# When feature blocks are loaded in a two-layer MLP by seven products, and the order of the last piece's copies, adds and squares

## The chip, the cores and the metric

The kernel runs on one core of one Trainium2 chip. The metric is the device time of one execution in microseconds (us); the figure given for a kernel is the median of its runs, and a separate execution is taken with the hardware profiler.

## What is computed

One inference step of a one-layer hybrid decoder trunk, for a prompt of 512 tokens and 8 sample tokens, 520 tokens in all, with D_MODEL = 2048. The change touches the last third of it, the MLP and the final norm:

```python
xm = rmsnorm(h, p['norm_mlp_g'])
h = h + jnp.square(jax.nn.relu(xm @ p['w_up'])) @ p['w_down']
...
y_prompt = rmsnorm(hp, final_norm_g)
y_sample = rmsnorm(hs, final_norm_g)
```

W_up is 2048 x 8192 and W_down 8192 x 2048, both float32. Ahead of it, and not touched, come the input projection, four mixers, W_out, cross attention and W_o.

## The kernel before, in words

**Precision.** A float32 product is made from three float32r products: each operand is split in a high part (ScalarE copies it to float32r: `whi`, `xbh`) and a low part (VectorE subtracts the high part from the operand: `wlo`, `xbl`), and TensorE runs high by high, low by high and high by low.

**The down stage.** The hidden features are cut in eight chunks p of 1024 features (`N_CHUNK`), and the 2048 outputs in four strips g of 512 (`GROUPS`). One group G = 4p + g multiplies one chunk by one strip, so there are 32 groups (`N_GROUP`). In a group both matrices are seen as 2 x 2 quarters, and seven products of sums of quarters (`down_product(G, o)`, o = 0 to 6, 24 matmuls each, 168 in a group) take the place of eight. The four quarters of the result are called corners; they are collected in `cbuf`, and GpSimd's queue adds a finished group to `hscr` in HBM with an accumulating DMA (not for the last chunk, whose groups are added on the chip).

**Feature blocks.** The sums of quarters of the hidden features are the same for the four groups of a chunk. They lie in HBM (`hidd`), seven blocks of 520 KB in a chunk, one for each product. `load_block(p, k)` (L903) loads block k of chunk p on SP's queue to one of two sets of buffers (set p % 2). `block_hi` (L1657, ScalarE) makes its high part, `block_lo` (L3330, VectorE) its low part. In chunk p these splits are made for chunk p + 1: block 0 in the group g = 0, blocks 1 and 2 in g = 1, 3 and 4 in g = 2, 5 and 6 in g = 3 (the lists `blocks`, L1710 and L3378). A set may be written once the products of the chunk two before are done with it.

**Weight pieces.** Each group needs four quarters of its piece of W_down, `load_down(G, r)` (L919), 512 KB each, in `raw` for even groups and in `odd` for odd ones. SP's loop (L960) loads the pieces of G + 2 during group G: quarters 0 and 2, then blocks, then quarters 3 and 1. Each load waits until its buffer is free, and SP takes them strictly in the order of the program.

**Order in a group.** TensorE (`period`, L2434) runs in group G: product 2, 3, 4 of G, product 0 of G + 1, products 5 and 6 of G, product 1 of G + 1. Product 4 needs ScalarE's `second_copy` (L1670, `u2d`), product 5 needs `third_copy` (L1677, `vd`) of what product 4 left in the same banks. The last group, G = 31, has no G + 1, so its product 5 stands right behind product 4. ScalarE (`period`, L1707) and VectorE (`period`, L3374) have their lists written out by hand; every wait holds all that stands behind it on that engine.

**The last chunk (p = 7, `end`).** `load_last(g)` fetches the sum so far, `hF[g]`, from HBM. For each half m = 0 to 7 of the strips VectorE adds the corners (`last_add(m)`, L3359), ScalarE squares the half to `sqa` and scales two tiles with the final gain (`last_half(m)`, L1695), and VectorE adds the squares to `sqb` (`last_square(m)`, L3369). Half 2g is the upper two tiles of strip g, which need the corners 11 and `corner_copy` (L1684); half 2g + 1 the lower two, which need `corner_21` (L3353), made from product 6. `final_sums` (L2462) sums `sqb` over features with matmuls by a column of ones; from it come the norm factors `rF`, then the transposed tiles are scaled to `ynat` and stored.

Of the kernel before, what the change touches and what calls it, by code (L numbers as in the profile page):

```python
# [21 lines left out]
P = 128  # L22
D = 2048
KT = D // P
# [142 lines left out]
def build(nc, io, consts_ap, outs):  # L167
# [33 lines left out]
    with ctx:  # L201
# [532 lines left out]
        def _(sp):  # L734
# [168 lines left out]
            def load_block(p, k):  # L903

                if p > 0:
                    sp.wait_ge(s.blk_lo, BLK_LO + 7 * (p - 1) + k + 1)
                if p < 2:
                    if p == 0 and k < 2:
                        sp.wait_ge(s.pe_unit, U_UP)
                        sp.wait_ge(s.s_sum, 2 * KF)  # L910
                    else:
                        sp.wait_ge(s.pe_unit, up_n(N_QUAD - 1, ((0, 0, 0, 0, 2, 6, 6), (3, 3, 4, 4, 5, 5, 2))[p][k]) + 1)
                else:
                    sp.wait_ge(s.pe_unit, down_n(GROUPS * (p - 1) - 1, k) + 1)
                for i in range(2):
                    sp.wait_ge(st_out[i], ST_OUT[i] + 32 * (QUADS // 2) * (p + 1))
                sp.dma_start(xbl[p % 2][k][:].bitcast(F32), hidd[p, :, HID_BLOCK[k], :, :]).then_inc(blk_in[k], 16)
# [39 lines left out]
            load_down(1, 3)  # L957
            load_block(0, 5)
            load_block(0, 6)
            for G in range(N_GROUP):  # L960
                p, g = G // GROUPS, G % GROUPS
                if G + 2 < N_GROUP:
                    load_down(G + 2, 0)
                    load_down(G + 2, 2)
                if p + 1 < N_CHUNK:
                    for k in ((0, 1, 2), (3, 4), (5, 6), ())[g]:
                        load_block(p + 1, k)
                if G + 2 < N_GROUP:
                    load_down(G + 2, 3)
                    load_down(G + 2, 1)  # L970
# [82 lines left out]
        def _(act):  # L1053
# [548 lines left out]
            def hi_down(G, o):  # L1602

                if o in (0, 1, 6):
                    act.wait_ge(*down_in(G, {0: 0, 1: 3, 6: 1}[o]))
                else:
                    act.wait_ge(s.s_sum, SUMS + 4 * G + {2: 2, 3: 3, 4: 1, 5: 4}[o])
                high(down_n(G, o), down_source(G, o))
# [86 lines left out]
            def last_half(m):  # L1695

                g, i = m // 2, m % 2
                act.wait_ge(s.f_add, F_ADD + m + 1)
                if m >= 2:
                    act.wait_ge(s.ss_done, 4 * KT + m - 1)  # L1700
                act.activation((sqb if m == 0 else sqa)[:], hF[g][:, 2 * i:2 * i + 2, :], ACT.Square).then_inc(s.sq_done, 1)
                act.wait_ge(s.sq_done, 4 * KT + m + 1)
                for t in (2 * i, 2 * i + 1):
                    act.activation(hF[g][:, t, :], hF[g][:, t, :], ACT.Copy,
                                   scale=gains[:, 5, 4 * g + t:4 * g + t + 1]).then_inc(s.f_ev, 1)

            def period(G):  # L1707

                p, g = G // GROUPS, G % GROUPS
                blocks = [7 * (p + 1) + k for k in ((0,), (1, 2), (3, 4), (5, 6))[g]] if p + 1 < N_CHUNK else []  # L1710
                end, more = p == N_CHUNK - 1, G + 1 < N_GROUP
                hi_down(G, 4)
                if G == 0:
                    store(QUADS + N_QUAD - 1)
                if end:
                    load_last(g)
                    if g > 0:
                        last_half(2 * g - 2)
                second_copy(G)
                if more:  # L1720
                    hi_down(G + 1, 0)
                if G == 0:
                    block_hi(5)
                else:
                    for j in blocks[0:1]:
                        block_hi(j)
                hi_down(G, 5)
                if G == 0:
                    block_hi(6)
                if end and g > 0:  # L1730
                    last_half(2 * g - 1)
                third_copy(G)
                hi_down(G, 6)
                if more:
                    first_copy(G + 1)
                    hi_down(G + 1, 1)
                for j in (blocks if G == 0 else blocks[1:2]):
                    block_hi(j)
                corner_copy(G)
                if more:  # L1740
                    hi_down(G + 1, 2)
                    hi_down(G + 1, 3)
# [49 lines left out]
        def _(pe):  # L1792
# [669 lines left out]
            def final_sums():  # L2462

                pe.wait_ge(s.ss_done, 4 * KT + 7)
                for t in range(5):
                    n = P if t < 4 else NS
                    for i in range(2):
                        mm = pe.matmul(lin[0:n, 3, t:t + 1], sqb[:, i, P * t:P * t + n], ones[:, 0:1], start=i == 0, stop=i == 1)
                mm.then_inc(s.stat_mm, 1)

            for m, (c, t) in enumerate(turned_units):
# [18 lines left out]
        def _(v):  # L2490
# [876 lines left out]
                                ALU.add).then_inc(s.f_add, 1)  # L3367

            def last_square(m):  # L3369
                if m > 0:  # L3370
                    v.wait_ge(s.sq_done, 4 * KT + m + 1)
                    tt(sqb[:], sqb[:], sqa[:], ALU.add, s.ss_done)

            def period(G):  # L3374

                p, g = G // GROUPS, G % GROUPS
                end, more = p == N_CHUNK - 1, G + 1 < N_GROUP
                blocks = [] if end else [7 * (p + 1) + k for k in ((0,), (1, 2), (3, 4), (5, 6))[g]]  # L3378
                corner_11(G)
                down_sum(G, 4)  # L3380
                lo_down(G, 4)
                if end and g > 0:
                    last_add(2 * g - 1)
                if more:
                    lo_down(G + 1, 0)
                    down_sum(G + 1, 1)
                if G == 0:
                    block_lo(5)
                else:
                    for j in blocks[0:1]:  # L3390
                        block_lo(j)
                lo_down(G, 5)
                if G == 0:
                    block_lo(6)
                if end and g > 0:
                    last_square(2 * g - 2)
                corner_22(G)
                lo_down(G, 6)
                if more:
                    down_sum(G + 1, 2)  # L3400
                    lo_down(G + 1, 1)
                if end and g > 0:
                    last_square(2 * g - 1)
                if more:
                    down_sum(G + 1, 3)
                    lo_down(G + 1, 2)
                corner_21(G)
                if more:
                    lo_down(G + 1, 3)
                for j in (blocks if G == 0 else blocks[1:2]):  # L3410
                    block_lo(j)
                if end:
                    last_add(2 * g)

            for p in range(QUADS):
# [101 lines left out]
```

## Time and profile before

| | before |
|---|---|
| median of 3 runs | 2715.56 us (2714.91 to 2715.73) |
| the profiled execution's own time | 2713.25 us |
| its span, first to last instruction | 2710.6 us |
| TensorE matmul busy | 2651.4 us, 98% |
| VectorE busy | 1770.5 us, 65% |
| ScalarE busy | 1099.5 us, 41% |
| GpSimd busy | 650.9 us, 24% |
| DMA | 458.68 MB, mean 169 GB/s |
| mean granted TensorE clock | 0.991 of full speed |

The down stage lies from about 2014 us of the span to 2683 us, the end of the kernel behind it. A busy share of TensorE near 100% says that there are few gaps, not that the array is at its peak. The clock is 1.00 where the full 2.4 GHz is granted and 0.50 where half of it, 1.2 GHz, is.

### The profile page before, as it was taken

Reading aid. Unit: us, or ns where it says so; the run is one execution under the profiler, and the core shown is the slowest. Engines: PE = TensorE matmul, PEld = TensorE weight load, DVE = VectorE, ACT = ScalarE, POOL = GpSimd, SP = SyncE. Lnnn points to the kernel's source line nnn. Section 1 sums busy time; section 2 is a strip of 40 time slices with the busy share of each in tenths; the row PEclk is TensorE's granted clock in tenths of the full one; section 3 lists DMA queues with packets and bytes.
Section 4 is the critical chain, followed back from the end, with each engine's and each line's share of the span. In section 5 each row is a group of like instructions: output and inputs, shape, how many; then the busy total and the mean of one; then the engine's idle time right before and its main releaser. Section 6 shows DMA issues by size and latency. Waiting matters only on the chain.

```text
span 2710.6 us, 50301 instructions
## 1 busy us (share of the span) xinstructions
PE 2651.4 (98%) x20814; PEld 2534.1 (93%) x20814; DVE 1770.5 (65%) x2261; ACT 1099.5 (41%) x1411; POOL 650.9 (24%) x320
## 2 busy tenths in 40 slices
PE   9999999999999999999999999999999999999997
PEld 7999998777999988779999999999999999999997
DVE  4686944766522343432287878888788887888786
ACT  5312124535322211222234545555455454555555
POOL 1545434676444322334400000000000000000000
PEclk9999999999999999999999999999999999999998
DMA  6743445565533556543337877777887777777762
GB/s 188 143 105 101 106 121 172 148 192 160 182 93 93 159 192 202 187 134 118 114 115 192 213 194 210 207 201 207 219 248 193 205 200 196 198 190 214 200 172 89
DMA packets 522264, 458.68 MB, mean 169 GB/s; under 512 B 34633, under 2 KB 455343, under 8 KB 520111
## 3 DMA queue, kind: packets, MB, share of 16 engines
q1 hardware_dynamic: 442680, 338.53, 42.6%
q10 hardware_dynamic: 67739, 72.86, 8.8%
q0 software_dynamic: 11648, 44.50, 8.4%
q8 instruction: 143, 2.34, 0.4%
q14 instruction: 54, 0.44, 0.0%
HBM read 357.78 MB, written 83.66 MB: 163 GB/s over the span
## 4 chain that ended last, share of the span: by engine, by line
PE 76%; issue 7%; DVE 6%; POOL 4%; DMA 4%; ACT 2%; SPq 1%; POOLq 0%; ACTq 0%; DVEq 0%
PE lin L1812 30%; PE aux L2381 17%; PE lin L2416 11%; PE aux L2416 8%; PE lin L2381 3%; POOL wlo L1029 3%; DMA xbl<-hidd 2%; POOL wlo L987 2%; PE aux L2134 1%; PE aux L2089 1%; DVE turn L2494 1%; DVE wlo L3238 1%; PE lin L2029 1%; DMA raw<-in_w_in 1%; PE aux L2080 1%
## 5 line engine op out<-in xcount | busy, mean ns | idle before, releaser
L987 POOL TENSOR_TENSOR wlo<-raw,whi 128x1024 fp32r<-128x1024 f32 x176 | 432.5, 2461 | 659.2 <-ACT whi L1078 465.1
L1078 ACT ACTIVATE whi<-raw 128x1024 fp32r<-128x1024 f32 x140 | 147.6, 1058 | 448.5 <-PE lin L1812 313.0
L2416 PE MATMUL lin<-xbh,whi 128*128 128x260 f32 x1024 | 291.9, 285 | 16.5 <-issue 12.9
L2416 PE MATMUL lin<-xbl,whi 128*128 128x260 f32 x1024 | 291.3, 284 | 0.0
L2416 PE MATMUL lin<-xbh,wlo 128*128 128x260 f32 x1024 | 291.2, 284 | 0.0
L1812 PE MATMUL lin<-xh,whi 128*128 128x260 f32 x896 | 257.3, 287 | 0.0
L1812 PE MATMUL lin<-xl,whi 128*128 128x260 f32 x896 | 254.6, 284 | 0.0
L1812 PE MATMUL lin<-xh,wlo 128*128 128x260 f32 x896 | 254.3, 284 | 0.0
L3238 DVE TENSOR_TENSOR wlo<-raw,whi 128x1024 fp32r<-128x1024 f32 x176 | 214.8, 1221 | 31.3 <-ACT whi L1587 31.2
L1587 ACT ACTIVATE whi<-sums 128x1024 fp32r<-128x1024 f32 x166 | 175.1, 1055 | 147.7 <-DVE sums L3261 124.6
L1587 ACT ACTIVATE whi<-raw 128x1024 fp32r<-128x1024 f32 x176 | 185.7, 1055 | 89.2 <-PE aux L2381 78.2
L2416 PE MATMUL aux<-xbh,wlo 128*128 128x260 f32 x768 | 217.6, 283 | 0.0
L2416 PE MATMUL aux<-xbh,whi 128*128 128x260 f32 x768 | 217.1, 283 | 0.4 <-issue 0.4
L2416 PE MATMUL aux<-xbl,whi 128*128 128x260 f32 x768 | 217.2, 283 | 0.0
L3238 DVE TENSOR_TENSOR wlo<-sums,whi 128x1024 fp32r<-128x1024 f32 x166 | 202.8, 1222 | 16.2 <-ACT whi L1587 13.7
L2416 PEld LDWEIGHTS lin<-xbh,whi 128*128 128x128 f32 x1024 | 194.4, 190 | 18.4 <-issue 14.3
L2416 PEld LDWEIGHTS lin<-xbh,wlo 128*128 128x128 f32 x1024 | 195.1, 191 | 0.0
L2416 PEld LDWEIGHTS lin<-xbl,whi 128*128 128x128 f32 x1024 | 194.9, 190 | 0.0
L2381 PE MATMUL aux<-th,whi 128*128 128x260 f32 x672 | 189.9, 283 | 2.7 <-DVE wlo L3238 2.7
L2381 PE MATMUL aux<-th,wlo 128*128 128x260 f32 x672 | 189.8, 282 | 0.0
L2381 PE MATMUL aux<-mh,wlo 128*128 128x260 f32 x672 | 189.7, 282 | 0.0
L2381 PE MATMUL aux<-ml,whi 128*128 128x260 f32 x672 | 189.7, 282 | 0.0
(509 smaller groups left out, 8191.1 us busy)
## 6 DMA issues: line engine op xcount, KB each, us to landing
raw<-in_w_up SPq DMA_DIRECT2D x128, 512.0 KB, 5.0
raw<-in_w_down SPq DMA_DIRECT2D x64, 512.0 KB, 4.9
odd<-in_w_down SPq DMA_DIRECT2D x64, 512.0 KB, 4.0
raw<-in_w_in SPq DMA_DIRECT2D x60, 512.0 KB, 3.8
xbl<-hidd SPq DMA_DIRECT2D x56, 520.0 KB, 11.0
hscr<-cbuf POOLq DMA_DIRECT2D x28, 1040.0 KB, 13.1
hidd<-st ACTq DMA_DIRECT2D x32, 780.0 KB, 8.4
raw<-in_w_out SPq DMA_DIRECT2D x32, 512.0 KB, 3.9
```

Source lines behind the costliest of these rows:

```text
L987: pool.tensor_tensor(wlo[:, slot, :], raw[:, slot % 2, :], whi[:, slot, :].bitcast(F32), ALU.subtract).then_inc(s.w_lo, 1)
L1029: pool.tensor_tensor(wlo[:, slot, :], src, whi[:, slot, :].bitcast(F32), ALU.subtract).then_inc(s.w_lo, 1)
L1078: act.activation(whi[:, slot, :], raw[:, slot % 2, :], ACT.Copy).then_inc(s.w_hi, 1)
L1587: act.activation(whi[:, n % 4, :], src, ACT.Copy).then_inc(s.w_hi, 1)
L1812: mm = pe.matmul(lin[:, 2 * i + f, 0:HALF], w, x, start=(n == 0 and part == 0), stop=(n == KT - 1 and part == 2))
L2029: mm = pe.matmul(lin[:, 2 * i + f, 0:HALF], w, m[:, k, HALF * f:HALF * f + HALF], start=(k == 0 and part == 0), stop=(k == KT - 1 and part ...
L2080: mm = pe.matmul(aux[32 * j:32 * j + 32, 2, :], pTd[:, m, 32 * b:32 * b + 32], piece[:, j, m, :], start=(g == 0 and m == 0), stop=(g == 1 ...
L2089: mm = pe.matmul(aux[:, 2, 0:NMEM], q[:, f0 + d, P * tt:P * tt + P], kTh[:, d, :], start=(d == 0), stop=(d == 3))
L2134: mm = pe.matmul(aux[:, d % 2, :], vNh[:, m, P * d:P * d + P], pT[:, m, :], start=(m == 0), stop=(m == 1))
L2381: mm = pe.matmul(out, w, m[:, kk, :], start=(first and kk == 0 and part == 0), stop=(last and kk == KF - 1 and part == 2), skip_group_chec ...
L2416: mm = pe.matmul(down_bank(G, o)[:, pr, :], w, m[:, kk, :], start=(first and kk == 0 and part == 0), stop=(last and kk == 3 and part == 2) ...
L3238: v.tensor_tensor(wlo[:, n % 4, :], src, whi[:, n % 4, :].bitcast(F32), ALU.subtract).then_inc(s.w_lo, 1)
```

## The change

It has five parts.

1. SP's queue loads blocks 0 and 1 of a chunk one group sooner: for chunk 1 ahead of the loop over groups, for later chunks in the group g = 3 of the chunk before the one that splits them, between quarters 2 and 3 of the weight piece. The groups g = 0, 1, 2 then load blocks 2 and 3, 4 and 5, and 6, where they had loaded three, two and two.
2. ScalarE in the last chunk: `last_half(2g - 2)` moves behind `second_copy` and the split of the next group's piece 0, `last_half(2g - 1)` behind `third_copy`, the split of piece 6, `first_copy` and the split of piece 1.
3. VectorE in the last group: `last_add(6)`, the upper tiles, stands ahead of `corner_21` and no longer behind it.
4. VectorE's last sum of squares: the two halves of `sqb` are added to one before the wait for the last squares, and these are then added as two half-size operations.
5. `final_sums` has 10 matmuls in place of 20.

```diff
@@ SP's queue @@
             load_block(0, 5)
             load_block(0, 6)
+            load_block(1, 0)
+            load_block(1, 1)
             for G in range(N_GROUP):
                 p, g = G // GROUPS, G % GROUPS
                 if G + 2 < N_GROUP:
                     load_down(G + 2, 0)
                     load_down(G + 2, 2)
                 if p + 1 < N_CHUNK:
-                    for k in ((0, 1, 2), (3, 4), (5, 6), ())[g]:
+                    for k in ((2, 3), (4, 5), (6,), ())[g]:
                         load_block(p + 1, k)
+                if g == GROUPS - 1 and p + 2 < N_CHUNK:
+                    load_block(p + 2, 0)
+                    load_block(p + 2, 1)
@@ ScalarE, period @@
                 if end:
                     load_last(g)
-                    if g > 0:
-                        last_half(2 * g - 2)
                 second_copy(G)
                 if more:
                     hi_down(G + 1, 0)
+                if end and g > 0:
+                    last_half(2 * g - 2)
...
                 if G == 0:
                     block_hi(6)
-                if end and g > 0:
-                    last_half(2 * g - 1)
                 third_copy(G)
                 hi_down(G, 6)
                 if more:
                     first_copy(G + 1)
                     hi_down(G + 1, 1)
+                if end and g > 0:
+                    last_half(2 * g - 1)
@@ TensorE, final_sums @@
-                    for i in range(2):
-                        mm = pe.matmul(lin[0:n, 3, t:t + 1], sqb[:, i, P * t:P * t + n], ones[:, 0:1], start=i == 0, stop=i == 1)
+                    mm = pe.matmul(lin[0:n, 3, t:t + 1], sqb[:, 0, P * t:P * t + n], ones[:, 0:1], start=True, stop=True)
@@ VectorE, last_square @@
-                if m > 0:
+                if 0 < m < 2 * GROUPS - 1:
                     v.wait_ge(s.sq_done, 4 * KT + m + 1)
                     tt(sqb[:], sqb[:], sqa[:], ALU.add, s.ss_done)
+                if m == 2 * GROUPS - 1:
+                    tt(sqb[:, 0, :], sqb[:, 0, :], sqb[:, 1, :], ALU.add)
+                    v.wait_ge(s.sq_done, 4 * KT + m + 1)
+                    tt(sqb[:, 0, :], sqb[:, 0, :], sqa[:, 0, :], ALU.add)
+                    tt(sqb[:, 0, :], sqb[:, 0, :], sqa[:, 1, :], ALU.add, s.ss_done)
@@ VectorE, period @@
+                if not more:
+                    last_add(2 * g)
                 corner_21(G)
...
-                if end:
+                if end and more:
                     last_add(2 * g)
```

SP's queue in the groups G = 3 and G = 4 before (`odd` holds the piece of group 5, `raw` that of group 6, `xbl_82` to `xbl_85` are blocks 0 to 3 of chunk 2):

```order
L931 DMA odd_104<-in_w_down 128x4x256
L931 DMA odd_105<-in_w_down 128x4x256 x2
L931 DMA odd_104<-in_w_down 128x4x256
L931 DMA raw<-in_w_down 128x4x256
L931 DMA raw_66<-in_w_down 128x4x256
L917 DMA xbl_82<-hidd 128x1040
L917 DMA xbl_83<-hidd 128x1040
L917 DMA xbl_84<-hidd 128x1040
L931 DMA raw_66<-in_w_down 128x4x256
L931 DMA raw<-in_w_down 128x4x256
```

and in the changed kernel:

```order
L931 DMA odd_104<-in_w_down 128x4x256
L931 DMA odd_105<-in_w_down 128x4x256
L917 DMA xbl_82<-hidd 128x1040
L917 DMA xbl_83<-hidd 128x1040
L931 DMA odd_105<-in_w_down 128x4x256
L931 DMA odd_104<-in_w_down 128x4x256
L931 DMA raw<-in_w_down 128x4x256
L931 DMA raw_66<-in_w_down 128x4x256
L917 DMA xbl_84<-hidd 128x1040
L917 DMA xbl_85<-hidd 128x1040
L931 DMA raw_66<-in_w_down 128x4x256
L931 DMA raw<-in_w_down 128x4x256
```

Blocks 0 and 1 went from behind four weight loads to ahead of them, and block 3 came into group 4.

ScalarE in the last group, G = 31, before (L1675 is the second copy, L1682 the third, L1688 the corner copy, L1701 and L1704 are `last_half`):

```order
L1081 DMA hF_101<-hscr 128x2080
L1701 ACTIVATE sqa<-hF_100 128x1040
L1704 ACTIVATE hF_100<-hF_100,gains 128x520 x2
L1675 ACTIVATE u2d<-lin 128x520
L1587 ACTIVATE whi<-sums 128x1024
L1701 ACTIVATE sqa<-hF_100 128x1040
L1704 ACTIVATE hF_100<-hF_100,gains 128x520 x2
L1682 ACTIVATE vd<-lin 128x520
L1587 ACTIVATE whi<-odd_104 128x1024
L1688 ACTIVATE cbuf_97<-lin 128x2x260
```

and in the changed kernel:

```order
L1086 DMA hF_101<-hscr 128x2080
L1680 ACTIVATE u2d<-lin 128x520
L1706 ACTIVATE sqa<-hF_100 128x1040
L1709 ACTIVATE hF_100<-hF_100,gains 128x520 x2
L1592 ACTIVATE whi<-sums 128x1024
L1687 ACTIVATE vd<-lin 128x520
L1592 ACTIVATE whi<-odd_104 128x1024
L1706 ACTIVATE sqa<-hF_100 128x1040
L1709 ACTIVATE hF_100<-hF_100,gains 128x520 x2
L1693 ACTIVATE cbuf_97<-lin 128x2x260
```

Each block of a square and two scalings moved behind a copy that TensorE waits for; the second now stands right ahead of the corner copy. Lines are 5 higher for the same operation.

VectorE at the end of the last group, before (L3357 is `corner_21`, L3366 `last_add`, L2494 the sums of squares):

```order
L3357 TENSOR_TENSOR cbuf_97<-u2d,aux 128x2x260
L3366 TENSOR_TENSOR hF_101<-hF_101,cbuf_97 128x1040 x2
L2494 TENSOR_TENSOR sqb<-sqb,sqa 128x1040 x2
L3459 MEMSET rF 128x8
L2500 TENSOR_SCALAR rF<-lin 128x4
```

and in the changed kernel:

```order
L3370 TENSOR_TENSOR hF_101<-hF_101,cbuf_97 128x1040
L3361 TENSOR_TENSOR cbuf_97<-u2d,aux 128x2x260
L3370 TENSOR_TENSOR hF_101<-hF_101,cbuf_97 128x1040
L2498 TENSOR_TENSOR sqb<-sqb,sqa 128x1040
L2498 TENSOR_TENSOR sqb<-sqb 128x520
L2498 TENSOR_TENSOR sqb<-sqb,sqa 128x520 x2
```

One add of 1040 columns moved ahead of the corner, and the last sum of 1040 columns became three of 520.

## Rows read from the trace of the kernel before

**Rows 1.** The page, part 1: busy time of each engine
```profile
PE 2651.4 (98%) x20814; PEld 2534.1 (93%) x20814; DVE 1770.5 (65%) x2261; ACT 1099.5 (41%) x1411; POOL 650.9 (24%) x320
```
**Rows 2.** Who waited for whom, TensorE, whole span: total, times, longest us
```profile
PE lin L2416 <- issue: 12.9, 8, 2.7
...
PE lin L2468 <- DVE sqb L2494: 4.2, 1, 4.2
PE lin L2416 <- ACT vd L1682: 3.6, 2, 2.7
```
**Rows 3.** Who waited for whom, ScalarE, 2030 to 2600 us
```profile
ACT xbh L1661 <- DMA xbl<-hidd: 32.1, 6, 6.2
```
**Rows 4.** Timeline of SP's queue: start us, us, operation, count
```profile
2078.73 16.56 SPq L931 DMA_DIRECT2D odd<-in_w_down  x4
2098.88 4.05 SPq L931 DMA_DIRECT2D raw<-in_w_down  x2
2103.10 2.56 SPq L917 DMA_DIRECT2D xbl<-hidd  x3
...
2598.09 16.55 SPq L931 DMA_DIRECT2D raw<-in_w_down  x4
```
**Rows 5.** Timeline of ScalarE and VectorE: start us, us, operation, idle before
```profile
2025.48 1.06 ACT L1661 ACTIVATE xbh<-xbl 128x1040 fp32r<-128x1040 f32 x1
2114.18 1.07 ACT L1661 ACTIVATE xbh<-xbl 128x1040 fp32r<-128x1040 f32 x1 [6.20 <-DMA xbl<-hidd]
...
2109.16 1.22 DVE L3270 TENSOR_TENSOR sums<-odd,odd 128x1024 f32<-128x1024 f32 x1
```
**Rows 6.** DMA issues of 2014-2017, 2102-2106, 2018-2598 us: count, KB, us to landing
```profile
xbl<-hidd SPq DMA_DIRECT2D x2, 520.0 KB, 5.3
xbl<-hidd SPq DMA_DIRECT2D x3, 520.0 KB, 12.1
odd<-in_w_down SPq DMA_DIRECT2D x56, 512.0 KB, 4.0
```
**Rows 7.** One group as a window: PE, PEld, DVE, ACT, POOL busy, PEclk, DMA share, GB/s
```profile
2122.84:2142.16 19.32, 19.32 (x163) 19.32 (x162) 15.89 (x15) 10.68 (x13) 1.20 (x1) 1.00 0.81 222
```
**Rows 8.** Timeline of TensorE, behind gaps; then windows: PE busy (x), PEclk, DMA, GB/s
```profile
2117.77 0.36 PE L2416 MATMUL lin<-xbh,whi 128*128 128x260 f32 x1 [2.74 <-issue]
2655.33 0.39 PE L2416 MATMUL lin<-xbh,whi 128*128 128x260 f32 x1 [0.87 <-ACT vd L1682]
2675.62 0.39 PE L2416 MATMUL lin<-xbh,whi 128*128 128x260 f32 x1 [2.75 <-ACT vd L1682]
2690.15 3.68 PE L2468 MATMUL lin<-ones,sqb 128*128 128x1 f32 x20 [4.17 <-DVE sqb L2494]
...
2284.00:2287.20 3.20, 3.20 (x17) 0.50 0.41 107
2650.00:2660.00 10.00, 9.13 (x77) 1.00 0.00 1
2676.50:2680.00 3.50, 3.50 (x18) 0.51 0.02 5
```
**Rows 9.** Timeline of ScalarE, last group
```profile
2672.63 1.07 ACT L1701 ACTIVATE sqa<-hF 128x1040 f32<-128x1040 f32 x1 [2.50 <-DVE sqb L2494]
2673.73 1.35 ACT L1704 ACTIVATE hF<-hF,gains 128x520 f32<-128x520 f32 x2
2674.99 0.58 ACT L1682 ACTIVATE vd<-lin 128x520 f32<-128x520 f32 x1
```
**Rows 10.** Timeline of VectorE, from the last product's end
```profile
2683.26 0.70 DVE L3357 TENSOR_TENSOR cbuf<-u2d,aux 128x520 f32<-128x520 f32 x1 [4.34 <-issue]
2683.88 2.39 DVE L3366 TENSOR_TENSOR hF<-hF,cbuf 128x1040 f32<-128x1040 f32 x2
2686.25 1.24 DVE L2494 TENSOR_TENSOR sqb<-sqb,sqa 128x1040 f32<-128x1040 f32 x1
2688.76 1.24 DVE L2494 TENSOR_TENSOR sqb<-sqb,sqa 128x1040 f32<-128x1040 f32 x1 [1.26 <-ACT sqa L1701]
```

## The prediction
> **What bounds the kernel now.** I read the page's busy shares first: TensorE is busy 98% of the span, VectorE 65% [rows 1]. So only TensorE's gaps, its clock, and what runs after its last product can give time back. Next I read TensorE's list of waits: of its gaps in the down stage, eight are put down to "issue" (12.9 us, the longest 2.7), two to ScalarE's third copy `vd` (3.6 us), and one of 4.2 us lies ahead of the final sums [rows 2]. "Issue" names no cause, so I looked at what the engines that feed TensorE did there. ScalarE waited six times for a block, 32.1 us together, 6.2 at most [rows 3]: the six are block 0 of the chunks 2 to 7. The first is issued at 2103.10 [rows 4], blocks take 12.1 us to land in that place [rows 6], and ScalarE, which takes block 0 early in the same group, stands still for 6.20 us until 2114.18 [rows 5]. Everything behind it on ScalarE is late, the split of piece 5 and the third copy among it, and TensorE's product 5 starts after a gap of 2.74 us at 2117.77 [rows 8]. The next five chunks show the same. That is the reason for the stage's losses.
>
> **The loss at the six chunk borders.** I measure it by SP's queue, which starts each group's loads at the same point. A group with no gap takes 2098.88 - 2078.73 = 20.15 us. From 2098.88 to 2598.09, 24 groups, it is 499.21 us [rows 4]; 24 x 20.15 = 483.6, so 15.6 us are lost at the six borders. This is more than the gaps because after some gaps the clock is at its lower level for a while: 17 matmuls in 3.20 us at a granted clock of 0.50 behind the third gap [rows 8], where a group's pace (168 in 20.15 us, 0.12 us each) would need 2.0.
>
> **Part 1, block loads.** The change issues block 0 and 1 in group g = 3, behind the first two weight loads. These start at 2078.73 and the matching pair at 2098.88 takes 4.05 us [rows 4], so the blocks go out at about 2083. With the landing of 12.1 us [rows 6] they are there at 2095; ScalarE wants block 0 at 2114.18 - 6.20 = 2107.98 [rows 5]. 13 us to spare: the wait goes wholly, and with it 15.6 us. What pays for it? (a) The queue: two more issues ahead of quarters 3 and 1 of group 5's piece. The loads were four in 16.56 us because they wait for free buffers, not for the queue; a pair of issues costs under 1 us of it (three took 2.56). (b) The rings: g = 3 now moves two blocks beside the accumulating DMA, as g = 1 does before. That group had a DMA share of 0.81 and no gap, 19.32 us of TensorE in 19.32 [rows 7]. Group g = 0 goes from three blocks to two. So no group carries more than one that already runs without a gap. (c) The added wait: block 1 waits for product 1 of group 4p + 3, and quarters 3 and 1 are queued behind. Quarter 1 goes out at about 2095 (2078.73 + 16.56) and VectorE first reads it at 2109.16 [rows 4, 5], 14 us later, against a landing of 4.0 [rows 6]. (d) Ahead of the loop, blocks 0 and 1 of chunk 1 join blocks 5 and 6 of chunk 0, which landed in 5.3 us [rows 6] after an issue between 2014 and 2017, so by 2022, and are taken from 2025.48 [rows 5]. Even if the two more doubled that landing it would cost 2 us at most; I take 0. The small gaps there (about 2 us) come from VectorE's backlog, and stay. Bounds of part 1: nothing below half of it, 8 us, if block 1 or a weight piece became late next; above, 16.5.
>
> **Part 2, ScalarE's order in the last chunk.** TensorE waited 0.87 us in group 30 and 2.75 us in group 31 for the third copy [rows 8]. In group 31 ScalarE ran a square and two scalings, 2672.63 to 2674.99, just ahead of the copy [rows 9]. In the new order the copy is free to start when product 4 ends. In group 30 product 0 of group 31 covers it: the gap goes. The matmul before a gap is counted to its modelled end, 0.28 us, where the pace is 0.12, so a gap costs 0.16 more than shown: 1.0 us. In group 31 nothing covers the copy: it takes 0.58, and the matmul followed 0.63 after its start, so a gap of about 0.7 stays of 2.75: 2.1 us. Behind the 2.75 gap the clock was at the lower level: 18 matmuls in 3.50 us at 0.51, at full pace 2.15; behind the 0.87 gap it stayed at 1.00 [rows 8]. With 0.7 left I count on 1.00, and 1.4 us. Product 5's low part must also be there: the split of piece 5 is now behind `last_half(4)`, which ends some 2.4 us (1.07 + 1.35, [rows 9]) after the second copy, and I get it ready 1 us before TensorE asks. The corner copy is late by about 1 us in groups 29 and 30, since 2.4 us of work now fill an idle time of 1.3; TensorE asks for what follows from it 2 us later. Nothing. Bounds of part 2: 0 (another wait takes the place) to 4.5.
>
> **Part 3, the upper tiles' add.** It was one of two adds, 2.39 us together, after `corner_21` [rows 10]; now it runs while product 6 (2.87 us) does. It needs the corner copy, which follows product 5 and `last_half(5)`: I get the add done 0.7 us before product 6 ends. Gain 1.15 us.
>
> **Part 4, squares.** The first half-size add runs while ScalarE squares; behind the wait stand two of 0.70 (the price of 520 columns, [rows 10]) for one of 1.24: a loss of 0.15 us.
>
> **Part 5, final sums.** 20 matmuls took 3.68 us [rows 8]; 10 take half: 1.8 us. TensorE's clock there could be the one or the other level: 0.9 to 2.8.
>
> **Sum:** 15.6 + 1.0 + 2.1 + 1.4 + 1.15 - 0.15 + 1.8 = 22.9 us. The profiled execution's own time, 2713.25, becomes 2690.4. The median of the runs lies 2.3 us higher, 2715.56, and I take the same difference: 2692.7 us, 0.84% less.
>
> **A rule weighed.** After the gaps of 2.75 and of the third border the clock was at 1.2 GHz for over 3 us, after 0.87 it was at 2.4 GHz [rows 8]. The Trainium skill, "TensorE: Matmul & The Clock Gate", section "Part 1: The HAM clock gate", says that half rate is the default and that activity releases it; by that, the 0.7 us still left in group 31 could cost the lower clock again. That is rival A.
>
> **The rivals.**
> A. The clock falls in group 31 all the same. For it: the gap does not vanish. Against: a longer one, 0.87, left it alone. The 1.4 us stay: 2694.1.
> B. The last piece moves its wait. VectorE is dense there, and its list has ScalarE's squares behind one more split; if the low part of piece 5 or 6, or the upper add, comes late by what was gained, parts 2 and 3 give nothing, and 15.6 + 1.8 - 0.15 = 17.3 are left: 2698.3.
> C. The borders give half: block 0 comes in time, but VectorE or block 2, issued in the same group as before, is next in line. Block 2 is wanted in g = 1, a group later, which speaks against it. 7.8 less: 2700.5.
> D. It doesn't do what it says: the moved loads are held in the queue by the wait for product 1 and land where they did. Only the last piece's 7.3 us are left, or less: 2708 to 2712.
> E. Slower. Beside the accumulating DMA, the two moved blocks delay quarter 1 of the piece of group 4p + 5, so that VectorE stands at its sum. It decides from a landing over 14 us (2109.16 - 2095) where 4.0 is shown; at 20 us, six times 6 us are lost where 22.9 are won: 2728. The Trainium skill, "DMA: Bandwidth & Descriptors", section "Queues, rings and completion order", has each DMA engine take packets from its queues in turn, so that a load does share with GpSimd's DMA; the 12.1 us of a block beside that DMA against 5.3 without [rows 6] agrees. But a group with the same load ran without a gap [rows 7].
>
> **How the numbers follow.** About 0.2% (5.4 us) is what a measurement of this kernel can tell from no change. Chances: forecast 0.70, A 0.10, B 0.09, C 0.05, D 0.04, E 0.02. D lies half on each side of the bound. Faster 0.95, same 0.03, slower 0.02. The likely range takes in A, B and most of C, the unknown clock of part 5 and the runs' spread: 2688.5 to 2701.
>
> **What would show it.** ScalarE's waits for `xbl` gone and no "issue" gap after 2030; 24 groups in about 483.6 us; third copy right behind product 4 in the groups 30 and 31; the upper add ended before `corner_21` starts; final sums in 1.8 us. It is wrong if the groups at the borders still take over 20.3 us, if SP's weight loads or VectorE's sums show a new DMA wait in g = 0, or if the gap in group 31 is over 1 us.

## The result and the profile after

The changed kernel takes 2689.97 us (median of 4 runs, 2687.57 to 2693.34) against 2715.23 us of the kernel before, in 4 runs too. The estimated ratio is 0.9916, 95% interval 0.9903 to 0.9929: 23 us less, between 19 and 26. (The two medians by themselves are 25.3 us apart, within that interval.) In a later comparison, with more runs, it came out as 0.9915 (e10, below). 2692.7 had been forecast.

| | before | after |
|---|---|---|
| median | 2715.23 us | 2689.97 us |
| profiled execution's own time | 2713.25 us | 2693.34 us |
| span | 2710.6 us | 2691.2 us |
| TensorE matmul busy | 2651.4 us | 2649.5 us |

The two profiled executions differ by 19.9 us only, less than the medians. The reason is in a part that the change does not touch: the first gap of the down stage ends at 2025.41 after, at 2020.88 before, 4.5 us later for the same instructions. All numbers below are therefore differences inside the stage. From the end of that gap to the end of the span it is 2710.6 - 2020.9 = 689.7 us before and 2691.2 - 2025.4 = 665.8 us after: 23.9 less, where 22.9 had been summed up.

TensorE's waits after, from the list of who waited for whom (engine, line, releaser: us in total, times, longest); they answer to [rows 2]:

```profile
PE lin L2472 <- DVE sqb L2498: 3.3, 1, 3.3
...
PE lin L2421 <- issue: 1.5, 2, 0.9
...
PE lin L2421 <- ACT vd L1687: 0.7, 1, 0.7
```

The six "issue" gaps at the chunk borders are gone. The 1.5 us that are left are two of the small gaps at the start of the stage, which were there before. ScalarE's list has no line for `xbl` any more, where it had 32.1 us [rows 3]. SP's queue in the timeline of the changed kernel (start us, us, operation, count), against [rows 4]:

```profile
2083.29 4.05 SPq L931 DMA_DIRECT2D odd<-in_w_down  x2
2087.50 0.89 SPq L917 DMA_DIRECT2D xbl<-hidd  x2
2089.82 10.04 SPq L931 DMA_DIRECT2D odd<-in_w_down  x2
2103.44 4.04 SPq L931 DMA_DIRECT2D raw<-in_w_down  x2
...
2586.64 16.56 SPq L931 DMA_DIRECT2D raw<-in_w_down  x4
```

Blocks 0 and 1 go out 4.2 us into the group before, and the next weight loads keep their place. From 2103.44 to 2586.64, 24 groups, it is 483.20 us, 20.13 a group, where it had been 499.21: 16.0 us. The six gaps before (2.74, 1.42, 2.02, 1.35, 1.58 and 2.27 us) add up to 11.4 us, 12.3 with the 0.16 that a modelled end hides at each; most of the rest is the clock behind two of them, those of 2.02 and 2.27 us, where the granted clock was 0.67 and 0.70 over the next 3 us. Behind the other four, the longest among them, it was 1.00. The group g = 3 as a window (busy and records of PE, PEld, DVE, ACT, POOL, then clock, DMA share, GB/s), against [rows 7]:

```profile
2083.29:2103.44 20.15, 20.15 (x170) 20.15 (x169) 17.17 (x16) 11.09 (x14) 1.20 (x1) 1.00 0.77 211
```

It carries two blocks more than the group g = 3 before did: a DMA share of 0.77 and 211 GB/s, where it had been 0.64 and 158 from 2078.73 to 2098.88. TensorE is busy throughout. The end of the stage, from TensorE's timeline, against [rows 8]:

```profile
2660.94 0.39 PE L2421 MATMUL lin<-xbh,whi 128*128 128x260 f32 x1 [0.69 <-ACT vd L1687]
2672.96 1.40 PE L2472 MATMUL lin<-ones,sqb 128*128 128x1 f32 x10 [3.25 <-DVE sqb L2498]
```

and VectorE's, against [rows 10]:

```profile
2664.92 1.24 DVE L3370 TENSOR_TENSOR hF<-hF,cbuf 128x1040 f32<-128x1040 f32 x1 [0.67 <-ACT cbuf L1693]
2666.99 0.69 DVE L3361 TENSOR_TENSOR cbuf<-u2d,aux 128x520 f32<-128x520 f32 x1 [0.82 <-PE aux L2421]
2667.72 1.24 DVE L3370 TENSOR_TENSOR hF<-hF,cbuf 128x1040 f32<-128x1040 f32 x1
2668.88 1.23 DVE L2498 TENSOR_TENSOR sqb<-sqb,sqa 128x1040 f32<-128x1040 f32 x1
2670.15 0.70 DVE L2498 TENSOR_TENSOR sqb<-sqb 128x520 f32<-128x520 f32 x1
2671.38 1.43 DVE L2498 TENSOR_TENSOR sqb<-sqb,sqa 128x520 f32<-128x520 f32 x2 [0.53 <-ACT sqa L1706]
```

There is one gap for the third copy, 0.69 us, and none in group 30. The upper add runs from 2664.92 to 2666.16, and VectorE then waits 0.82 us for product 6: it is off the path. The pieces, each between two marks of its own trace:

| piece | before | after | gained | forecast |
|---|---|---|---|---|
| 24 groups (SP's marks) | 499.21 | 483.20 | 16.0 | 15.6 |
| from there to the end of group 31's gap | 77.53 | 74.30 | 3.2 | 3.1 |
| to `corner_21` (product 5's pace, the clock) | 7.64 | 6.05 | 1.6 | 1.4 |
| to the final sums (adds, squares) | 6.89 | 5.97 | 0.9 | 1.0 |
| final sums, to VectorE's next | 3.79 | 1.51 | 2.3 | 1.8 |

### The profile page after: what moved, and what is told of

It is laid out like the page before. It is cut to its first block, busy times and chain, and to the rows that moved or that the text cites. A ratio compares the mean times of both kernels' runs of the same rounds, so it can differ in the third digit from the quotient of the medians.

```text
span 2691.2 us, 50284 instructions
## 1 busy us (share of the span) xinstructions
PE 2649.5 (98%) x20804; PEld 2532.2 (94%) x20804; DVE 1774.4 (66%) x2263; ACT 1099.5 (41%) x1411; POOL 651.7 (24%) x320
## 4 chain that ended last, share of the span: by engine, by line
PE 83%; issue 6%; DVE 5%; POOL 4%; ACT 1%; DMA 1%; SPq 0%; POOLq 0%; DVEq 0%; ACTq 0%
PE lin L1817 31%; PE aux L2386 18%; PE lin L2421 14%; PE aux L2421 10%; PE lin L2386 3%; POOL wlo L1034 3%; POOL wlo L992 1%; PE aux L2094 1%; PE aux L2139 1%; DVE turn L2498 1%; PE lin L2034 1%; PE aux L2085 1%; PE lin L1907 1%; DVE rot L2498 0%; PE aux L1984 0%
## 5 line engine op out<-in xcount | busy, mean ns | idle before, releaser
L2386 PE MATMUL aux<-tl,whi 128*128 128x260 f32 x672 | 190.3, 283 | 0.0
```

What stands on the lines that cost most here:

```text
L2386: mm = pe.matmul(out, w, m[:, kk, :], start=(first and kk == 0 and part == 0), stop=(last and kk == KF - 1 and part == 2), skip_group_chec ...
```

## The experiments

My theory: block 0 of each chunk was issued too late, because it stood in SP's queue behind two weight loads that wait for their buffers; nothing else was wrong at the borders, and the last piece is a separate matter whose parts add up. The rivals: shared bandwidth or a burst of three blocks as the cause; gains of the last piece that are only a matter of the clock; a new wait of the weight loads if more is moved.

### One half of the change at a time

e1: the kernel before with part 1 alone.

```diff
+            load_block(1, 0)
+            load_block(1, 1)
...
-                    for k in ((0, 1, 2), (3, 4), (5, 6), ())[g]:
+                    for k in ((2, 3), (4, 5), (6,), ())[g]:
                         load_block(p + 1, k)
+                if g == GROUPS - 1 and p + 2 < N_CHUNK:
+                    load_block(p + 2, 0)
+                    load_block(p + 2, 1)
```

> The kernel before with part 1 alone (the block loads a group ahead). My theory: ScalarE's six waits for block 0 were the whole loss at the borders, so 24 groups take 483.2 us instead of 499.2 and the median falls by 16 us, to about 2699; the last chunk stays as it was (gaps of about 0.9 and 2.7 us for the third copy, 4.2 us ahead of the final sums). Rival (the gain needs the last piece's new order too, or was partly chance between runs): less than 12 us.

2695.28 us against 2714.01, ratio 0.9928 (0.9915 to 0.9941). In its SP timeline the group marks are these:

```profile
2100.54 4.05 SPq L931 DMA_DIRECT2D raw<-in_w_down  x2
...
2583.74 16.56 SPq L931 DMA_DIRECT2D raw<-in_w_down  x4
```

483.20 us again, and TensorE's timeline keeps the end as it was:

```profile
2640.97 0.39 PE L2421 MATMUL lin<-xbh,whi 128*128 128x260 f32 x1 [0.87 <-ACT vd L1687]
2661.27 0.39 PE L2421 MATMUL lin<-xbh,whi 128*128 128x260 f32 x1 [2.78 <-ACT vd L1687]
2674.25 3.72 PE L2473 MATMUL lin<-ones,sqb 128*128 128x1 f32 x20 [4.17 <-DVE sqb L2499]
```

So part 1 alone gives the 16.0 us. The median fell by 18.7, 2.7 more; the interval is 16 to 23 us, with the 16.0 at its lower end. In the profiled execution 1.5 us more came from the clock, which stayed at 1.00 behind the gap of 2.78 us (from 2661.50 to 2665.00) where it had fallen before; this is no effect of part 1 that these runs could show.

e2: the kernel before with parts 2 to 5, as in the diff of the change.

> The kernel before with parts 2 to 5 alone. My theory: the parts add up without touching each other, so the six border gaps stay (the 24 groups take some 499 us) and the end gives 8 us (3.2 + 1.6 for the copies and the clock, 0.9 for the adds, 2.3 for the final sums): about 2707. Rival (the end gains only because it is entered without the earlier gaps): under 4 us.

2704.23 us against 2714.01, ratio 0.9957 (0.9943 to 0.9972). ScalarE's list of waits from 2040 to 2600 us still has the blocks:

```profile
ACT xbh L1661 <- DMA xbl<-hidd: 32.2, 6, 6.5
```

and the 24 groups take 2599.49 - 2098.81 = 500.68 us. The end shows the gap of 0.69 us and none in group 30. By the marks of the table above the last piece gives 3.2, 1.6, 0.9 and 1.7 us here, where the changed kernel has 3.2, 1.6, 0.9 and 2.3; the 0.6 are in the final sums, which met a lower clock (below). So the two halves do not touch each other: the borders' gaps did not help or hide anything at the end.

### Why block 0 was late

e3: block 0 alone goes a group ahead; the groups load (1, 2), (3, 4), (5, 6).

```diff
+            load_block(1, 0)
...
-                    for k in ((0, 1, 2), (3, 4), (5, 6), ())[g]:
+                    for k in ((1, 2), (3, 4), (5, 6), ())[g]:
                         load_block(p + 1, k)
+                if g == GROUPS - 1 and p + 2 < N_CHUNK:
+                    load_block(p + 2, 0)
```

> The kernel before with block 0 alone moved a group ahead; the groups g = 0, 1, 2 still load blocks 1 and 2, 3 and 4, 5 and 6. My theory: only block 0 was late, so this gives the same 16 us as part 1 whole (median about 2699), no wait of ScalarE for xbl. Rival (the burst of blocks with the accumulating DMA was too much, and block 1 or 2 is next in line): a wait for xbl in g = 1 and less than 12 us.

2693.80 us, ratio 0.9923 (0.9909 to 0.9936); from 2100.59 to 2583.79, 483.20 us, and no wait for `xbl`. Moving block 1 as well was worth nothing that these runs show.

e4: block 0 stays in the group g = 0, but at its head.

```diff
+                if p + 1 < N_CHUNK and g == 0:
+                    load_block(p + 1, 0)
                 if G + 2 < N_GROUP:
                     load_down(G + 2, 0)
                     load_down(G + 2, 2)
                 if p + 1 < N_CHUNK:
-                    for k in ((0, 1, 2), (3, 4), (5, 6), ())[g]:
+                    for k in ((1, 2), (3, 4), (5, 6), ())[g]:
```

> The kernel before, block 0 stays in the group g = 0 but stands ahead of the two weight loads instead of behind them. SP has issued its last weight load of the group before at about 2095 and waits there for a buffer until 2098.9, while the block's own buffer has long been free: so block 0 should go out at about 2095.3, 8 us sooner, and land before the 2108.0 at which ScalarE asks if it takes no more than 12.7 us. My theory (place in the queue is all): no wait or under 1 us, 13 to 16 us gained. Rival (shared bandwidth: it now competes with a weight load, GpSimd's DMA and the next two weight loads): it lands 3 us or more too late and the gain is under 10 us.

2696.67 us, ratio 0.9935 (0.9921 to 0.9948), the same within the scatter as e1 and e3. SP's timeline:

```profile
2075.75 16.56 SPq L931 DMA_DIRECT2D odd<-in_w_down  x4
2092.47 0.38 SPq L917 DMA_DIRECT2D xbl<-hidd  x1
2095.90 4.04 SPq L931 DMA_DIRECT2D raw<-in_w_down  x2
2100.11 2.19 SPq L917 DMA_DIRECT2D xbl<-hidd  x2
...
2579.10 16.56 SPq L931 DMA_DIRECT2D raw<-in_w_down  x4
```

Two places in the queue are enough: block 0 goes out 3.4 us before its group's first weight load, and the groups take 2579.10 - 2095.90 = 483.20 us. In the query for this one block its time to landing is

```profile
DMA to landing us min/median/max: 5.2/5.2/5.2
```

and ScalarE takes it without a wait:

```profile
2103.95 1.05 ACT L1589 ACTIVATE whi<-odd 128x1024 fp32r<-128x1024 f32 x1
2104.90 1.07 ACT L1663 ACTIVATE xbh<-xbl 128x1040 fp32r<-128x1040 f32 x1
```

It landed at 2097.7, 7.2 us before ScalarE took it. Against the kernel before, where it landed 15.3 us after the group's first weight load (2114.18 - 2098.88) and not 1.8, that is 13.5 us sooner. 7.6 of them come from the issue, 3.4 us ahead of that weight load and not 4.2 behind it; 5.9 come from the landing, 5.2 us and not 11.1 (2114.18 - 2103.10), since GpSimd's accumulating DMA of the group went out at 2099.05, behind it. So the rival was half right about the hardware and wrong about this cure: beside GpSimd's DMA a block takes twice as long to land, but it now goes ahead of that DMA, and the earlier issue alone is already more than the wait of 6.2 us. (No run takes GpSimd's DMA away, so that it is what doubles the landing is argued, from the places where blocks land fast and slow.) The Trainium skill, "DMA: Bandwidth & Descriptors", section "Queues, rings and completion order", has each DMA engine take packets from its queues in turn, and the two landings agree with it.

e8: the changed kernel with three blocks in g = 3.

```diff
+            load_block(1, 2)
...
-                    for k in ((2, 3), (4, 5), (6,), ())[g]:
+                    for k in ((3, 4), (5, 6), (), ())[g]:
...
+                    load_block(p + 2, 2)
```

> The changed kernel with three blocks (0, 1 and 2) loaded in g = 3, then blocks 3 and 4 in g = 0 and 5 and 6 in g = 1. Block 2 waits for TensorE's product 2 of the same group, 2.9 us after product 1, and weight quarters 3 and 1 stand behind it in SP's queue. This looks for the slower rival's mechanism: 1.5 MB of blocks beside the accumulating DMA and the queue held. My theory (a margin of over 10 us on the weight quarters, block 0 no longer pressed): same time as the changed kernel within 2 us. Rival E: quarter 1 lands late, VectorE waits for it at its sum in g = 0, a gap at each border, and 5 us or more are lost.

2688.43 us, ratio 0.9903 (0.9888 to 0.9918), the changed kernel's within the intervals. SP's timeline:

```profile
2077.51 4.05 SPq L931 DMA_DIRECT2D odd<-in_w_down  x2
2081.72 3.69 SPq L917 DMA_DIRECT2D xbl<-hidd  x3
2085.51 8.57 SPq L931 DMA_DIRECT2D odd<-in_w_down  x2
2097.66 4.04 SPq L931 DMA_DIRECT2D raw<-in_w_down  x2
...
2580.86 16.56 SPq L931 DMA_DIRECT2D raw<-in_w_down  x4
```

Block 2 does hold the queue: the two weight loads go from 2089.82 - 2083.29 = 6.5 us into the group to 8.0. But the pair still ends at the same point of the group, because its second load waits for its buffer anyway. 483.20 us: the slower rival's mechanism has no hold even with half as much again moved.

### The last piece

e5: the kernel before with part 2 alone, ScalarE's order.

> The kernel before with part 2 alone, ScalarE's order in the last chunk. My theory: the gap in group 30 goes (1.0 us), that of group 31 shrinks from 2.75 to 0.7 (2.1 us) and the clock stays at 2.4 GHz behind it (1.4 us): 4.5 us. Rival A (the clock falls behind a gap of 0.7 us as well): 3 us, and a granted clock near 0.5 for over 3 us behind that gap.

2708.34 us against 2712.80, ratio 0.9986 (0.9977 to 0.9995): 4.5 us by the medians, 1.4 to 6.2 by the interval. TensorE has one gap there:

```profile
2673.98 0.39 PE L2416 MATMUL lin<-xbh,whi 128*128 128x260 f32 x1 [0.69 <-ACT vd L1682]
```

and the clock behind it, as a window (us, PE busy and records, granted clock, DMA share, GB/s):

```profile
2674.50:2678.00 3.50, 3.50 (x31) 1.00 0.02 5
```

Rival A does not show: behind a gap of 0.69 us the clock was at 2.4 GHz, here and in the changed kernel. But the converse is not so sure as I took it. Five profiled executions have the long gap in group 31, 2.75 to 2.79 us. From its end to `corner_21` it took 6.10 us in e1 and in e3, as fast as with the short gap (6.05), 7.35 in e6, 7.64 before and 8.86 in e4. So a gap of this length was followed by 0 to 2.8 us lost to the clock, differently in each execution, and the 1.4 us that I booked are one draw of it.

e6: the kernel before with parts 3, 4 and 5 alone.

> The kernel before with parts 3, 4 and 5 alone: the upper tiles' add, the squares in one half, ten matmuls. My theory: 1.0 us up to the final sums and 1.8 to 2.3 us in them, about 3 us in all. In this kernel the 2.75 us gap in group 31 and the low clock behind it stay, and the corner copy is late by as much, so that the upper add may no longer end before the corner: then 2 us. Rival (the ten matmuls were fast only because the clock was high in that run): they take 1.8 us instead of 1.4 where the clock is low.

2710.46 us against 2712.80, ratio 0.9992 (0.9982 to 1.0003): too little to tell from nothing in the medians. In the trace VectorE has the upper add done by 2680.53 and `corner_21` starts at 2681.35, so the add is off the path although ScalarE's order is the old one, and 5.98 us later come the final sums, as in the changed kernel (5.97; 6.89 before):

```profile
2687.33 1.96 PE L2467 MATMUL lin<-ones,sqb 128*128 128x1 f32 x10 [3.26 <-DVE sqb L2493]
```

Ten records took 1.96 us here and 1.40 in the changed kernel. (In these traces a float32 matmul leaves two records: the source has ten matmuls before and five after, and where the list of the change and the prediction say 20 and 10 they count records.)

e7: the changed kernel with parts 4 and 5 undone.

```diff
-                if 0 < m < 2 * GROUPS - 1:
+                if m > 0:
                     v.wait_ge(s.sq_done, 4 * KT + m + 1)
                     tt(sqb[:], sqb[:], sqa[:], ALU.add, s.ss_done)
...
-                    mm = pe.matmul(lin[0:n, 3, t:t + 1], sqb[:, 0, P * t:P * t + n], ones[:, 0:1], start=True, stop=True)
+                    for i in range(2):
+                        mm = pe.matmul(lin[0:n, 3, t:t + 1], sqb[:, i, P * t:P * t + n], ones[:, 0:1], start=i == 0, stop=i == 1)
```

> The changed kernel with parts 4 and 5 undone: one add of 1040 columns at the end, 20 matmuls in the final sums. It tells count from clock. In the changed kernel 10 matmuls took 1.40 us (0.14 each) where 20 had taken 3.68 (0.18 each). If a higher clock gave the extra 0.4 us and still holds here, 20 take 2.8 us and the kernel loses 1.4 us less 0.15 against the changed one; if the pairs themselves are slow, or the clock falls within them, they take 3.7 and it loses 2.1 us.

2690.61 us, ratio 0.9918 (0.9904 to 0.9931), not to be told from the changed kernel. The trace does tell:

```profile
2668.03 2.85 PE L2473 MATMUL lin<-ones,sqb 128*128 128x1 f32 x20 [3.06 <-DVE sqb L2499]
```

and the window of these matmuls

```profile
2668.00:2670.90 2.90, 2.87 (x21) 0.67 0.00 0
```

Twenty in 2.85 at a clock of 0.67, ten in 1.40 at 0.73, ten in 1.96 and twenty in 3.68 at 0.50 and 0.51: the time goes by count and by clock. Halving the count is worth 1.4 us (this kernel against the changed one) to 1.7 us (e6 against before); the rest of the 2.3 us in the changed kernel's trace was the clock. Part 4 alone can be read here too: from `corner_21` to the final sums it is 5.78 us with the one add of 1040 columns and 5.97 with the two of 520, a loss of 0.2 where 0.15 had been worked out.

e10: the changed kernel once more.

> The changed kernel again, unchanged, to set its time beside the kernel before on one chip in more runs and to see which parts of its time repeat. My theory: the 24 groups between the borders (483.2 us) and the path behind the last product repeat to 0.2 us, while the time at which the down stage begins moves by some us from run to run (it did by 7.5 us over the kernels so far, whose code up to there is the same), and the final sums take 1.4 or 2.0 us with the clock. Rival (the gain itself varies): the groups differ by more than 1 us.

2689.68 us against 2714.03, ratio 0.9915 (0.9901 to 0.9928). The groups take 2582.81 - 2099.61 = 483.20 us, the gap in group 31 is 0.69 us, from `corner_21` to the final sums it is 5.97 us, and these take 1.22 at a granted clock of 0.83, less than either value expected. The first gap of the down stage ends at 2021.59; over the kernels of this study, whose code up to there is the same, it lay between 2017.87 (e4) and 2026.85 (e9). Behind it the two profiled executions of the changed kernel took 665.8 and 665.5 us. So the scatter of some us between runs comes mostly from the stretch ahead of the down stage.

e9: can the last adds leave the chain? The final sums in three passes.

```diff
-                    tt(sqb[:, 0, :], sqb[:, 0, :], sqb[:, 1, :], ALU.add)
-                    v.wait_ge(s.sq_done, 4 * KT + m + 1)
-                    tt(sqb[:, 0, :], sqb[:, 0, :], sqa[:, 0, :], ALU.add)
-                    tt(sqb[:, 0, :], sqb[:, 0, :], sqa[:, 1, :], ALU.add, s.ss_done)
+                    tt(sqb[:, 0, :], sqb[:, 0, :], sqb[:, 1, :], ALU.add, s.ss_done)
...
-                for t in range(5):
-                    n = P if t < 4 else NS
-                    mm = pe.matmul(lin[0:n, 3, t:t + 1], sqb[:, 0, P * t:P * t + n], ones[:, 0:1], start=True, stop=True)
+                for i, x in enumerate((sqb[:, 0, :], sqa[:, 0, :], sqa[:, 1, :])):
+                    if i == 1:
+                        pe.wait_ge(s.sq_done, 4 * KT + 2 * GROUPS)
+                    for t in range(5):
+                        n = P if t < 4 else NS
+                        mm = pe.matmul(lin[0:n, 3, t:t + 1], x[:, P * t:P * t + n], ones[:, 0:1], start=i == 0, stop=i == 2, skip_group_check=True)
```

> The changed kernel with the last squares never added by VectorE: five matmuls sum the half with all earlier squares while ScalarE squares the last tiles, and ten more sum the two tiles of sqa into the same columns as soon as they are there. It leaves VectorE's two adds (1.43 us) out of the chain behind the last square and keeps ten matmuls in it. My theory: 1.4 us less between the last square and rF, seen in the trace, too little for the medians (0.05%). Rival (the ten matmuls fall to the lower clock, since TensorE has then waited between the five and the ten): 1.96 us instead of 1.40 and 0.9 us gained.

2692.79 us, ratio 0.9926 (0.9912 to 0.9939): no gain, a miss. As it turned out, this kernel loses squares of the first pass from the prompt tokens' norm (e11 tells why); its instructions, and so its time, are those of the full sum. Its TensorE timeline:

```profile
2672.44 1.15 PE L2475 MATMUL lin<-ones,sqb 128*128 128x1 f32 x10 [1.28 <-DVE sqb L2501]
2673.52 2.90 PE L2475 MATMUL lin<-ones,sqa 128*128 128x1 f32 x20
```

I had counted ten records behind the last square and there are 20. From the last square's start to VectorE's first work on `rF` it is 2676.53 - 2671.65 = 4.88 us, where the changed kernel has 2674.47 - 2670.21 = 4.26: 2.90 us of matmuls took the place of 1.43 of adds and 1.40 of matmuls, and they began late, behind the ten records of the first pass.

e11: one start flag for the five columns.

```diff
-                        mm = pe.matmul(lin[0:n, 3, t:t + 1], x[:, P * t:P * t + n], ones[:, 0:1], start=i == 0, stop=i == 2, skip_group_check=True)
+                        mm = pe.matmul(lin[0:n, 3, t:t + 1], x[:, P * t:P * t + n], ones[:, 0:1], start=i + t == 0, stop=i == 2, skip_group_check=True)
```

> The kernel of e9 (final sums in three passes over five columns of one bank) with the start flag on the very first matmul alone, where each of the five columns had one. Theory: a start flag empties the whole bank's running sums and not only the column written, so that in e9 the columns 0 to 3 lost the first pass (all squares but the last strip's lower tiles) and only column 4, the samples, kept it; then one start gives the norm of all tokens. Rival: a column's sum does not survive the pause between the passes; then nothing changes. The time is that of e9: TensorE has 20 records of matmuls behind the last square (a float32 matmul leaves two) where the changed kernel has 10 behind two adds, so neither gains.

One execution, 2690.45 us. With the flag on the first matmul alone all tokens have their full sum; in e9 the samples, whose column is the last to be started, had theirs and the prompt tokens had not. The start flags are all that differs, so a later column's flag cost earlier columns of the bank their first pass, and the pause between the passes did no harm. The theory's "empties" says too much, though. In the changed kernel, too, each of the five columns has a start flag of its own, nothing is added behind it, and all five sums are right. So the stored sum stays; what the flag changed is that the next matmul onto an earlier column no longer added to it. Whether all of the prompt tokens lost the whole first pass no run shows.

## Why the prediction was right

- **What bounds the kernel, the loss at the borders.** Right. Reading the six "issue" gaps through ScalarE's waits led to block 0, and e3 and e4 show that block 0 alone was late. The 24 groups took 498.95 to 500.68 us in four kernels with the late block and 483.20 in nine without; 15.6 had been taken from a gapless group of 20.15, and the mean group is 20.13.
- **Part 1.** The blocks went out at 4.2 us into the group and no wait took their place. Block 0 landed 11.0 us after it went out at 2087.50, at 2098.5, and ScalarE took it at 2112.43: 13.9 us to spare, where 13 had been worked out. (a) to (c) held: quarters 3 and 1 went out at 2089.82, the pair took 10.04 us, and from 2040 to 2600 no engine waited for any DMA. The landing of 4.0 that (c) set against its 14 us needs care. The trace has no landing for those two loads; in the twelve of the 24 groups that load `raw`, quarter 1 landed in 3.9 to 4.5 us, but quarter 3, which goes out beside GpSimd's DMA, in 10.0 to 12.4. (c) is right because quarter 1 is the last load of a group, not because every weight lands in 4. (d) held: the three small gaps at the stage's start are 0.61, 0.43 and 0.89 us, as before. Taking g = 1 as the model for the loaded g = 3 was sound: 222 GB/s there, 211 here; e8 shows that the margin was larger than argued.
- **Part 2.** Right in both gaps: 0.69 us left where "about 0.7" stood. The corner copy's delay did no harm. The clock term, 1.4 us, was right for this pair of executions (1.6), but e1 and e3 show that it is no fixed price.
- **Parts 3 and 4.** 0.9 us together, where 1.0 stood. The upper add ended 0.8 us before `corner_21` began; 0.7 had been worked out.
- **Part 5.** The term that was furthest off: 1.8 forecast, 2.3 measured in this pair. e6 and e7 show 1.4 to 1.7 for the count, a little under the half of 3.68, and the rest is the clock, as the bounds allowed. That the two nearly meet is luck of the clock: in e2 the same edit gave 1.7.
- **The sum.** 22.9 forecast for the stage, 23.9 in the two traces. The median, 2689.97, is 2.7 below 2692.7: 1.0 of it from the terms, and the rest lies within what the untouched first 2020 us vary from run to run. For the same reason the profiled execution's own time, 2693.34, missed its forecast of 2690.4 on the other side.
- **The rivals.** A: not seen, the clock stayed up behind 0.69 us in eight executions (after, e2, e5, e7, e8, e9, e10 and e11, by the time to `corner_21`, 6.04 to 6.11 us). B: no wait moved. C and D: fell with 483.20 us. E: fell with e8; what was not tried is a load heavy enough to make a weight quarter late.

## What to carry to other kernels

When the busiest engine's gaps are put down to nothing, read the waits of the engines that feed it at the same moments. Here one of them waited for a DMA to land, and the queue that issued it showed what it stood behind; moving that one load proved it the cause. In an in-order DMA queue, a load whose buffer has long been free should not stand behind loads that wait for theirs; two places were worth as much here as a whole group of lead. And measure such an edit between marks inside its stage: the 24 groups took 483.20 us in all nine kernels without the late block (498.95 to 500.68 in the four with it), while the whole kernel moved by several.

## What the runs showed of the hardware

- A 520 KB block landed in 5.2 us ahead of GpSimd's accumulating DMA of 1040 KB (e4) and in 9.7 to 13.1 us in the places of the changed kernel, beside it. Weight loads of 512 KB show the same: 11.8 us beside it (`raw`, out at 2110.00), 4.1 us for the last of that group, out at about 2119.6. That sharing is the cause is argued, not tried.
- After a gap of 2.7 to 2.8 us TensorE's clock fell to 1.2 GHz in some executions and not in others: before it did (18 matmuls in 3.50 us [rows 8]), in e1 the granted clock was 1.00 behind a gap of 2.78 us. Nor does the length of the gap order it: at the borders before, the clock stayed at 1.00 behind 2.74 us and fell behind 2.02 and 2.27. What decides it is open. Behind 0.69 us it did not fall in any of eight executions.
- Behind a matmul with a start flag, the next matmul onto another column of the same PSUM bank replaced the sum there and did not add to it (e9 and e11), while a sum that was only read afterwards was intact (the changed kernel). The Trainium skill, "PSUM — Partial Sum Buffer", section "PSUM: the matmul accumulator", says that a second group's first matmul clears the first group's state in the bank, on the blocks of 32 partitions that its output touches, so that the first group's next matmul overwrites; these two kernels agree for the bank and do not test the partitions.
